# Inverting the delta rule's triangular blocks on GpSimd by back substitution instead of on TensorE by levels

## The reference

```
N_t = strict triangle of (decay * beta * k k^T), 128 x 128, one per head and tile
U_t = inverse of (I + N_t)
u   = U_t @ (beta * v - carried part);  out = masked (q k^T) @ u + carried part
```

## Time and profile before

| | |
|---|---|
| median of 3 runs | 2574.83 us (2574.62 to 2575.49) |
| profiled execution: its time / its span | 2578.98 us / 2576.8 us |
| PE busy | 2524.3 us (98%) |
| PE weight loads | 2079.9 us (81%) |
| DVE / ACT / POOL busy | 1454.3 (56%) / 1201.4 (47%) / 202.6 us (8%) |
| DMA | 426.5 MB, mean 166 GB/s |
| mean granted TensorE clock | 0.992 |

### The profile page before, as it was taken

How to read it: one execution, slowest core, us unless ns; L and a number is a source line. 1 busy time by engine, 2 the same in 40 slices (tenths; PEclk the granted TensorE clock), 3 DMA queues, 4 the chain that set the end, 5 groups by cost and what they waited for, 6 DMA issues and landing times.

```text
span 2576.8 us, 29757 instructions
## 1 busy us (share of the span) xinstructions
PE 2524.3 (98%) x12194; PEld 2079.9 (81%) x12194; DVE 1454.3 (56%) x1735; ACT 1201.4 (47%) x1670; POOL 202.6 (8%) x147
## 2 busy tenths in 40 slices
PE   8999999999999999999999999998999999999998
PEld 7878887987888788888876777777888888888886
DVE  6654665465456545556674544456655545456675
ACT  5533454254245433545555434445544444445654
POOL 0033003201310131000010000000000000000000
PEclk9999999999999999999999999999999999999999
DMA  6542454244335433555656544424655556555553
GB/s 220 178 148 99 147 180 147 99 157 153 115 126 169 153 125 128 192 199 201 211 169 209 169 147 133 147 104 158 212 190 186 195 180 196 186 190 196 180 191 135
DMA packets 221000, 426.53 MB, mean 166 GB/s; under 512 B 13782, under 2 KB 16111, under 8 KB 220866
## 3 DMA queue, kind: packets, MB, share of 16 engines
q1 hardware_dynamic: 213248, 411.72, 48.1%
q10 hardware_dynamic: 7618, 12.93, 1.5%
HBM read 420.39 MB, written 4.23 MB: 165 GB/s over the span
## 4 chain that ended last, share of the span: by engine, by line
PE 61%; issue 32%; DVE 3%; ACT 2%; DMA 1%; POOL 1%; ACTq 0%; SPq 0%; POOLq 0%; DVEq 0%
PE gemm L1290 16%; PE gemm L1292 16%; PE gemm L1291 16%; PE side L866 2%; PE side L1003 2%; PE side L993 2%; PE side L1008 1%; DVE arena L1680 1%; DVE weight_lo L1680 1%; PE side L1212 1%; DMA arena<-x 1%; POOL stats L2199 1%; PE side L968 1%; ACT weight_hi L1312 0%; PE side L1247 0%
## 5 line engine op out<-in xcount | busy, mean ns | idle before, releaser
L1680 DVE TENSOR_TENSOR weight_lo<-weight_raw,weight_hi 128x1024 fp32r<-128x1024 f32 x780 | 975.8, 1252 | 824.6 <-ACT weight_hi L1312 824.0
L1312 ACT ACTIVATE weight_hi<-weight_raw 128x1024 fp32r<-128x1024 f32 x780 | 821.7, 1055 | 799.0 <-PE gemm L1292 778.9
L1290 PE MATMUL gemm<-weight_hi,x_hi 128*128 128x512 f32 x2368 | 957.0, 404 | 0.0
L1292 PE MATMUL gemm<-weight_hi,x_lo 128*128 128x512 f32 x2368 | 929.2, 392 | 0.0
L1291 PE MATMUL gemm<-weight_lo,x_hi 128*128 128x512 f32 x2368 | 926.8, 391 | 0.0
L1290 PEld LDWEIGHTS gemm<-weight_hi,x_hi 128*128 128x128 f32 x2368 | 447.9, 189 | 97.3 <-issue 11.5
L1292 PEld LDWEIGHTS gemm<-weight_hi,x_lo 128*128 128x128 f32 x2368 | 447.1, 189 | 97.5
L1291 PEld LDWEIGHTS gemm<-weight_lo,x_hi 128*128 128x128 f32 x2368 | 448.1, 189 | 89.4 <-issue 2.4
L1290 PE MATMUL gemm<-weight_hi,lhs_hi 128*128 128x512 f32 x736 | 289.6, 393 | 8.4 <-DVE lhs_lo L1680 8.4
L1291 PE MATMUL gemm<-weight_lo,lhs_hi 128*128 128x512 f32 x736 | 287.1, 390 | 0.0
L1292 PE MATMUL gemm<-weight_hi,lhs_lo 128*128 128x512 f32 x736 | 287.1, 390 | 0.0
(11 more groups left out here) (185 smaller groups left out, 1365.7 us busy)
## 6 DMA issues: line engine op xcount, KB each, us to landing
weight_raw<-in_w_in_dram SPq DMA_DIRECT2D x207, 1024.0 KB, 5.1
weight_raw<-in_w_out_dram SPq DMA_DIRECT2D x48, 1024.0 KB, 5.1
weight_raw<-in_w_gate_dram SPq DMA_DIRECT2D x44, 1024.0 KB, 5.1
weight_raw<-in_w_up_dram SPq DMA_DIRECT2D x44, 1024.0 KB, 5.1
weight_raw<-in_w_down_dram SPq DMA_DIRECT2D x44, 1024.0 KB, 5.0
arena<-rel_line ACTq DMA_DIRECT2D x8, 384.0 KB, 7.7
arena<-in_x_dram SPq DMA_DIRECT2D x4, 512.0 KB, 9.5
arena<-in_x_dram ACTq DMA_DIRECT2D x4, 512.0 KB, 6.0
```

What stands on the lines that cost most here:

```text
L1290: e.matmul(pair[i][:, :], xh[:, s], wh, start=first, stop=False)
L1292: m = e.matmul(pair[i][:, :], xl[:, s], wh, start=False, stop=last)
L1312: return e.activation(o, i, ACT.Copy, scale=scale)
L1680: return e.tensor_tensor(o, x, y, op)
```

## The change

The 32x32 diagonal blocks of I + N are inverted on POOL by back substitution, one column after another. The blocks are stored to HBM from their 32-partition stripes (`nout`, 8 DMAs), read back so that each of the 32 blocks of a group lies flat in a partition, four times over (`nin`, one DMA of 512 KB); partition q*32+n solves 8 of block n's 32 columns (`dinv`: 31 pairs of a multiply and a subtract, each waiting for the one before by POOL's own semaphore, and a transposing copy). The result goes back to HBM (`tout`, 4 DMAs) and from there into the diagonal of a zeroed `Tt` (`tin`, 4 DMAs). All these DMAs are issued by SP, between the weight loads. PE transposes `Tt` to U (`dT`, now slot s+24) and does only the steps to width 64 and 128, in slots s+25 to s+28, with operands cut to the blocks. The levels' masks, and `dlev0`, are gone; `phase_constants` shrinks from 8 to 4 times 128 columns and its first load to 64 KB. `dsc` product 4 comes before product 2. DVE's subtractions for width 64 are four instructions on 32 partitions each. Below is the core of the diff (`...` stands for the matmul flags).

```diff
@@ side_table (slots; s = END of dz{g} + 1)
-        for q in range(6):
-            put(s + 8 + q, "dsc", g, q)
-        put(s + 14, "dlev0", g)
-        put(s + 16, "dT", g, 0), put(s + 16, "dT", g, 1)
-        for l in range(1, LEVELS):
-            put(s + 15 + 2 * l, "dX", g, l), put(s + 16 + 2 * l, "dY", g, l)
+        for z, q in enumerate((0, 1, 4, 2, 3, 5)):
+            put(s + 8 + z, "dsc", g, q)
+        put(s + 11, "nout", g), put(s + 13, "nin", g), put(s + 13, "dinv", g)
+        put(s + 21, "tout", g), put(s + 22, "tin", g)
+        put(s + 24, "dT", g, 0), put(s + 24, "dT", g, 1)
+        for z, wd in enumerate(LEVELS):        # LEVELS = (64, 128), SUB = 32, NSUB = 4
+            put(s + 25 + 2 * z, "dX", g, wd), put(s + 26 + 2 * z, "dY", g, wd)
@@ sync_program
+        def nout(g):
+            e.dma_start(claim("S", g)[:, 0:SUB * SUB // 4], a["const_unit"][:, :]).then_inc(sem("dma:unit"), 16)
+            w.wait_ge(*at("dve:dsc", g, 4))
+            to = n_dram[g].rearrange("(i h b) r c -> i b r h c", i=2, h=HB)
+            B0, B1 = by_head(blk("B0", g)), heads(blk("PB", g), 0)
+            for b in range(NSUB):
+                s = slice(b * SUB, (b + 1) * SUB)
+                e.dma_start(to[0, b], B0[s, :, s]).then_inc(sem("dma:nout"), 16)
+                e.dma_start(to[1, b], B1[s, :, s]).then_inc(sem("dma:nout"), 16)
+        def nin(g):
+            w.wait_ge(*at("dma:nout", g))
+            src = bass.AP(tensor=n_dram.tensor, offset=g * 2 * HB * NSUB * SUB * SUB,
+                          ap=[[0, 4], [SUB * SUB, P // 4], [1, SUB * SUB]])
+            e.dma_start(claim("N", g), src).then_inc(sem("dma:nin"), 16)
+        def tout(g):
+            w.wait_ge(*at("pool:dinv", g))
+            to = t_dram[g].rearrange("n (c q) r -> q n c r", q=4)
+            S = blk("S", g)[:, 2 * SUB * SUB // 4:3 * SUB * SUB // 4].rearrange("p (c r) -> p c r", r=SUB)
+            for q in range(4):
+                e.dma_start(to[q], S[q * SUB:(q + 1) * SUB]).then_inc(sem("dma:tout"), 16)
+        def tin(g):
+            w.wait_ge(*at("dma:tout", g))
+            w.wait_ge(*at("pool:dinv:zero", g))
+            src = t_dram[g].rearrange("(n b) c r -> b c n r", b=NSUB)
+            Tt = units(blk("Tt", g))
+            for b in range(NSUB):
+                s = slice(b * SUB, (b + 1) * SUB)
+                e.dma_start(Tt[s, :, s], src[b]).then_inc(sem("dma:tin"), 16)
         x_load(0)
+        slot = -AHEAD
         for ci in range(CHUNKS):
+            while ci >= RAW and slot < 2 * (ci - RAW) - 1:
+                for name, *args in SIDE[slot]:
+                    if name in steps:
+                        steps[name](*args)
+                slot += 1
             if ci >= RAW:
                 w.wait_ge(sem("act:hi"), 2 * (ci - RAW) + 2)
                 w.wait_ge(sem("dve:lo"), 2 * (ci - RAW) + 2)
@@ tensor_program (dT now waits for dma:tin and transposes Tt)
+        def dX(g, wd):
+            Tt, hw = units(blk("Tt", g)), wd // 2
+            if wd < P:
+                w.wait_ge(*at("act:dT", g, 1))
+                p = open_bank("dX", g, wd)
+                for n in range(2 * HB):
+                    for t in range(0, P, wd):
+                        s = slice(t, t + wd)
+                        m = e.matmul(p[s, n * hw:(n + 1) * hw], unit_of(g, n)[s, s], Tt[s, n, t:t + hw], ...)
+            else:
+                w.wait_ge(*at("dve:dY", g, hw))
+                p = open_bank("dX", g, wd)
+                for n in range(2 * HB):
+                    m = e.matmul(p[hw:wd, n * hw:(n + 1) * hw], unit_of(g, n)[:, hw:wd], Tt[:, n, 0:hw], ...)
+            m.then_inc(sem("pe:dX"))
+        def dY(g, wd):
+            U, X, hw = units(blk("U", g)), blk("X", g), wd // 2
+            w.wait_ge(*at("act:dX", g, wd))
+            if wd < P:
+                p, p2 = open_bank("dY", g, wd, "U"), open_bank("dY", g, wd, "T")
+                for n in range(2 * HB):
+                    for t in range(0, P, wd):
+                        s, x = slice(t, t + wd), X[t:t + wd, n * hw:(n + 1) * hw]
+                        e.matmul(p[t:t + hw, n * hw:(n + 1) * hw], x, U[s, n, t + hw:t + wd], ...)
+                        m = e.matmul(p2[s, n * hw:(n + 1) * hw], U[s, n, s], x, ...)
+            else:
+                p, X = open_bank("dY", g, wd, "U"), X[:, X6:BLK]
+                for n in range(2 * HB):
+                    m = e.matmul(p[0:hw, n * hw:(n + 1) * hw], X[:, n * hw:(n + 1) * hw], U[:, n, hw:wd], ...)
+            m.then_inc(sem("pe:dY"))
@@ pool_program (level, dlev0, dX and dY go)
+        def dinv(g):
+            e.memset(claim("X", g), 0.0)
+            e.memset(claim("Tt", g), 0.0).then_inc(sem("pool:dinv:zero"))
+            N = blk("N", g).rearrange("p (r c) -> p r c", c=SUB)
+            U, tmp, V = (blk("S", g)[:, z * SUB * SUB // 4:(z + 1) * SUB * SUB // 4] for z in range(3))
+            U = U.rearrange("p (r c) -> p r c", r=SUB)
+            w.wait_ge(*at("dma:nin", g))
+            w.wait_ge(*at("dma:unit", g))
+            for j in range(SUB - 1, 0, -1):
+                n = SUB // 4 - j // 4
+                c = slice(j // 4, SUB // 4)
+                by = tmp[:, 0:j * n].rearrange("p (r c) -> p r c", c=n)
+                after(tt(by, over(N[:, 0:j, j], 2, n), over(U[:, j, c], 1, j), ALU.mult))
+                after(tt(U[:, 0:j, c], U[:, 0:j, c], by, ALU.subtract))
+            e.tensor_copy(V.rearrange("p (c r) -> p r c", r=SUB), U).then_inc(sem("pool:dinv"))
```

More of the change, by code:

```diff
@@ L73, in host_constants @@
     base = [(r == c), (r > c), (r <= c), np.ones((P, P))]
[L74 to L78, removed]
+    first = base + [np.where(c > r, NEG, 0.0)]
+    column = (P // SUB) * np.arange(SUB // 4)[None, None, :] + (np.arange(P) // SUB)[:, None, None]
+    unit = np.arange(SUB)[None, :, None] == column
     same = r // GL_C == c // GL_C
@@ L389 @@
     "conv": ("convturn", "convtap", "convsilu"),
-    "delta": ("dk", "dss", "dkscale", "dkc", "drhs", "ddecay", "dmask", "dsc", "dlev0", "dT", "dX", "dY", "dv", "du0",
+    "delta": ("dk", "dss", "dkscale", "dkc", "drhs", "ddecay", "dmask", "dsc", "dinv", "dT", "dX", "dY", "dv", "du0",
               "dbu", "du1", "do", "donorm", "dgate", "dout"),
@@ L402 @@
 SIGNALS = {
-    "pe": {"ddecay": ("rest", "a", "b", "c"), "dY": ("", "T"), "ggate1": ("", "r")},
+    "pe": {"ddecay": ("rest", "a", "b", "c"), "dY": ("",), "ggate1": ("", "r")},
     "act": {"gate1": ("tanh", "exp", ""), "ddecay": ("a", ""), "gsum": ("q", "k", "")},
     "dve": {"cols0": ("",), "nscale": ("mean", ""), "gate1": ("v", "z", "arg", "u", ""), "dss": ("", "ck"),
-            "dY": ("T", "U"), "donorm": ("mean", ""), "mscore": ("w", "den"), "msq": ("mean", ""),
+            "dY": ("",), "donorm": ("mean", ""), "mscore": ("w", "den"), "msq": ("mean", ""),
             "ggate1": ("v", ""), "gsum": ("end", "rest", ""), "gsq": ("mean", ""), "alog": ("b", "")},
-    "pool": {"dlev0": ("first", "", "zero")},
+    "pool": {"dinv": ("zero", "")},
 }
@@ L492, in block_table @@
         live(("PB", g), ("dsc", g, 4), ("pe:do", g, 1))
[L493 to L497, removed]
+        live(("N", g), ("nin", g), ("pool:dinv", g))
+        live(("S", g), ("nout", g), ("dma:tout", g))
+        live(("Tt", g), ("dinv", g), ("pe:dX", g, 128))
+        live(("U", g), ("dT", g, 0), ("pe:du1", g))
+        live(("X", g), ("dinv", g), ("pe:dY", g, 128))
         live(("bv", g), ("dv", g, 0), ("pe:du1", g))
@@ L674, in at @@
         if signal.startswith("dma:"):
-            return sem(signal), DMAS[signal]
+            return sem(signal), DMAS[signal] * (args[0] + 1 if args else 1)
         return sem(signal), ORDINAL[(signal,) + args]
-    DMAS = {"dma:rel0": 32, "dma:rel1": 16, "dma:ggate1": 64, "dma:const2": 16}
+    DMAS = {"dma:rel0": 32, "dma:rel1": 16, "dma:ggate1": 64, "dma:const2": 16,
+            "dma:nout": 128, "dma:nin": 16, "dma:unit": 16, "dma:tout": 64, "dma:tin": 64}
     def blk(*name):
@@ L838, in x_load, with claim @@
                         ).then_inc(sem(f"dma:x{n}"), 16)
+        def claim(*name):
+            for s in before_block(*name):
+                w.wait_ge(*s)
+            return blk(*name)
+        def nout(g):
[26 more added lines that the diff above has]
+                e.dma_start(Tt[s, :, s], src[b]).then_inc(sem("dma:tin"), 16)
+        steps = dict(nout=nout, nin=nin, tout=tout, tin=tin)
         x_load(0)
+        slot = -AHEAD
         for ci in range(CHUNKS):
+            while ci >= RAW and slot < 2 * (ci - RAW) - 1:
[3 more added lines that the diff above has]
+                slot += 1
             if ci >= RAW:
@@ L986, in dX @@
[L986 to L993, removed]
-            m.then_inc(sem("pe:dX"))
@@ L1345, in cols @@
         def cols():
-            load(cst2[:, :], a["const_first"][:, 4 * P:], "dma:phase_constants")
+            load(NEGM, a["const_first"][:, 4 * P:], "dma:phase_constants")
         def xturn(key, m):
```

136 lines of the change are left out of this document (54 added, 82 removed).

## The result

Predicted 2547 us (2504 to 2606) and faster with 0.62. Measured over ten runs each: 2582.85 us (2575.88 to 2588.51) after, 2575.16 us (2574.62 to 2577.58) before, a ratio of 1.0028 with a 95% interval of 1.0020 to 1.0037. The change makes the kernel slower by a little over the 0.2% that can be told. The time lies in the range, on the other side of the kernel before. The profiled execution of after is the fastest of its ten, 2575.88 us, against 2578.98 us for the one whose rows stand above: on that footing the forecast was 2551, and 25 us are missing.

A forecast was written before the change was run, and what follows sets the result against it. PE, busy 98% of the span, was taken to bound the kernel. Removed calls -122 us, added matmuls +24, wait and clock +70 gave -28: 2574.83 to 2547 us, range 2504 to 2606.

The forecast's parts named there:

- What it removes from PE: PE's side calls: three each in levels 1 to 5 and two in the last go; 30.5 us a group, 122 for four.
- What it adds on PE: Small matmuls of `dX` and `dY` 64 and 128 on PE: 6.0 us a group, 24 for four.
- Rival D: `dY` 64 on PE: TensorE stops at each operand shape change, 31 a group, 10.9 us; 2590 us, slower; 11%.
- When the inverse is there: PE's `dT`, due at 200.4: chain `nout`, `nin`, `dinv`, `tout`, `tin` ends at 214.5, so PE waits 14.1 us.
- B: `dinv` on POOL: a short instruction costs 0.20 us with its wait, so the wait nearly goes; 2507 us; 25%.
- C: `dinv` on POOL: fixed price decides, 0.50 us an instruction, PE waits 26.5 us a group; 2596 us, slower; 22%.
- the long stride: `dinv` on POOL reads N's columns at 128-byte steps: 1.3 us a group, 5 for four, on top of the sum.
- The clock behind the wait: PE after its wait at `dT`: granted clock 0.70 on average over 11 us, 3.3 us lost a group.
- The sum: Whole kernel: -122 + 24 + 70 = -28 us, from the median 2574.83 to 2547 us.
- SP: SP's queue holds one weight load for 10 us; PE's own wait covers it, since three buffers are full.

## Why the prediction was wrong, step by step

**What it removes from PE** (-30.5 us a group): borne out as far as it can be told. The grouped kernel with the substitution left out keeps the removal, the four calls at 4.9 us a group and waits of 2.9 us in all, and stands at 2477: 97 us below the kernel before beside it, where the prediction's -122 + 24 is -98 with the clock left aside.

**What it adds on PE** (6.0 us a group): this is the step that failed. The four calls take 1.05 + 7.37 + 1.08 + 1.07 = 10.6 us. Three of them cost 3.2, about as priced. `dY` 64 was priced at 64 x 0.034 = 2.2, with some 0.5 for the change of rows, and it took 7.4. The price was taken from a call of one width and used for one that changes its width 31 times. Rival D had the mechanism and the call; it got 11%, by the argument that one entry into a call of other width shows no hole, and its price was taken from a change of rows, 0.35 us, over twice what a change of width costs. Its sign, holes between single matmuls of `dY` 64, is what the trace shows. Grouping gives back 5.7 a group in the call.

The Trainium skill, TensorEngine Tiling (Array Packing), "Key Properties", says that changing the tiling mode, not just the tile, drains TensorE. The trace agrees: 0.12 to 0.15 us from the last instruction of one width to the first of the other, and nothing to be seen for going from rows 0 to 64 within one width. That what happens in this time is a drain, no run here shows.

**The clock behind `dY` 64** was in no sum. In all seven profiles with 31 changes, waits or not, the clock falls to its lower level 2.5 to 5.6 us after each of the four calls begins, for 6.8 or 10.2 us; in none of the 20 calls of the five profiles in which the order was grouped, halved or of one width. The two edits that cure the call and leave the wait alone give 25 to 29 us back: four times 5.4 to 5.7 from the call; the other 3 to 6 us are put down to this stretch.

**When the inverse is there.** `nout` was to land at 167.2 and `nin` at 172.5. `nin` was issued at 164.28 already, 2.9 early, and POOL began at 175.99, 3.5 late: 11.7 us stand where the prediction had 5.3. `nin` first stands behind the weight load, then moves at 100 GB/s. `dinv` was to take 31.6 us (172.5 to 204.1) and took 31.3 (175.99 to 207.26). Its parts agree as well; groups on POOL by form, short ones clean and one beside splits:

```profile
L2251 POOL TENSOR_TENSOR arena<-arena 128x31 f32<-128x31 f32 x2 | 1.5, 752 | 22.0 <-DMA arena<-delta_blocks 21.9
...
L2251 POOL TENSOR_TENSOR arena<-arena 128x72 f32<-128x72 f32 x2 | 0.6, 324 | 0.2
...
L2251 POOL TENSOR_TENSOR arena<-arena 128x8 f32<-128x8 f32 x2 | 0.4, 204 | 0.2
```

From 8 to 72 columns that is 1.9 ns a column and 0.19 us fixed, against 1.68 and 0.18; beside the splits 42 of them took the 24.0 us to 200, 0.57 each against 0.30 / 0.56 = 0.54, and the last 20 took 0.33 each. That decides against B and C. The 5 us for four groups that the prediction, by the Trainium skill, GPSIMD Engine Reference, "Performance pitfalls for Q7 kernels", would have added for the long stride are not seen. The multiplies read N at that step and the subtractions don't, and at the same size a multiply takes no longer: 300 and 304 ns for the last clean pair of 60 columns, 202 and 206 ns for the pair of 8. `tout` and `tin` took 9.4 us together (207.26 to 216.68) against 10.4. `dT` was due at 198.6, not 200.4: the half clock that the kernel before has at this group's `ddecay`, under the 178.29 that was carried forward, did not fall in this execution. The wait was 18.1 and not 14.1: it ended 2.2 later (3.5 for `nin`, less 0.3 and 1.0) and began 1.8 earlier.

**The clock behind the wait**: 3.3 us lost a group from rows 3. PE resumed at 216.7 and the clock at 220.4: 3.7 us of work at half speed, 1.9 lost. Smaller than forecast. Wait and clock together are 20.0 against 17.4.

**The sum.** A group: -30.5 + 10.6 + 18.1 + 1.9 + 1.9 = +2.0 us, in which the last 1.9 is the second stretch as it falls on the products of weights (3.9 us, from 233.6 to 237.5). Matched product by product, the two traces stand 2.0 to 2.4 us further apart behind each of the four groups, and 1.6 nearer at each `ddecay`. That closes the profiled pair. The missing 25 us are 4 x 4.6 on the calls, 4 x 2.6 on wait and clock, 4 x 1.9 for the second stretch, less 4 x 1.6 at `ddecay` and some 5 in the second layer, where stretches at the lower clock fell otherwise. What `ddecay` gains looks like chance: the other profiled execution of the same kernel has the drop there in the first group. The median lies 7 us higher again, by the clock of the other executions.

**SP.** The prediction said that PE's wait covers the load that SP holds back. True here, and it was the trap of the cure: with PE's wait gone the weights ran dry, 7 to 10 us a group.

## What to carry to other kernels

Price a sequence of small matmuls in the order in which it is issued: one that changes the stationary tile's width between products pays for each change, and its products on different rows no longer go side by side, so group by width, and look whether the clock falls behind it. When a step waits for another engine's long chain, move its whole tail later, and the steps that a DMA queue has to stand at as well; a wait inside the queue that also loads the weights is paid a second time as soon as the first is hidden. A chain on an idle engine costs little once it has slots enough: here 35 us of POOL for about 1 us of time a group. What is left comes from other steps that stand behind the chain on the same engine, so look at those too.

## What the hardware did that was not expected

- Between 32 and 64 stationary columns (float32, 64 rows, 32 moving columns) it is 0.12 us from the last instruction of one width to the first of the other, 0.15 us back, whether the run before had 2 or 4 instructions (0.12 behind 32, too). Without a change they go in pairs 7 ns apart, one pair every 31 ns at 32 columns and every 58 ns at 64.
- In the call that changes width 31 times, with TensorE counted busy throughout, the granted clock fell to 0.5 some 2.5 to 5.6 us after its start and stayed there for 6.8 to 10.2 us, in all 28 calls traced; with 15 changes or fewer it did in none of 20.
- A 512 KB load that reads 128 KB four times from HBM moved 100 GB/s with 0.27 of the DMA engines busy, and with a weight load beside it the two moved some 200 GB/s together, where weights alone went at 361.
